# A routing stage whose low parts of weights come from adding DMAs instead of VectorE and GpSimd subtractions

## The reference, cut to what matters

```python
q = (xi @ w_pq).reshape(TOK_BLOCK, PEER_HEADS, 2, PEER_DQ // 2)
s = jnp.einsum('thcd,hckd->thck', q, sub_keys)
top_s, top_i = lax.top_k(s, PEER_TOPK)
cand_s = (top_s[:, :, 0, :, None] + top_s[:, :, 1, None, :]).reshape(TOK_BLOCK, PEER_HEADS, -1)
cand_i = (top_i[:, :, 0, :, None] * N_KEYS + top_i[:, :, 1, None, :]).reshape(TOK_BLOCK, PEER_HEADS, -1)
best_s, pos = lax.top_k(cand_s, PEER_TOPK)
idx = jnp.take_along_axis(cand_i, pos, axis=-1)
gate = jax.nn.softmax(best_s, axis=-1)
act = jax.nn.gelu(jnp.einsum('td,thkd->thk', xi, u_tab[idx]))
return jnp.einsum('thk,thkd->td', gate * act, v_tab[idx])
```

## Time and profile before

| | |
|---|---|
| median of 3 runs | 2640.74 us |
| lowest, highest | 2639.67, 2644.12 us |
| the profiled execution, its own time | 2645.87 us |
| its span in the trace | 2644.1 us |
| PE busy, share of the span | 2438.6 us, 92% |
| DVE busy | 2082.8 us, 79% |
| ACT busy | 1139.4 us, 43% |
| POOL busy | 835.4 us, 32% |
| granted TensorE clock, mean | 0.969 |

### The profile page before, as it was taken

The page is one execution under the profiler, slowest core; times in us unless marked ns, Lnnn a source line. Parts: engine busy times, 40 slices in busy tenths (PEclk is TensorE's granted clock), DMA queues, the critical chain, the costliest instruction groups (busy, mean ns, idle before and its releaser), DMA issues.

```text
span 2644.1 us, 38573 instructions
## 1 busy us (share of the span) xinstructions
PE 2438.6 (92%) x14986; PEld 2175.7 (82%) x14986; DVE 2082.8 (79%) x3567; ACT 1139.4 (43%) x1934; POOL 835.4 (32%) x559
## 2 busy tenths in 40 slices
PE   5889999998989978998995897999999999999997
PEld 4778888897878867998995786888888888888886
DVE  3667777733777674545999987999999999999999
ACT  4335565634656654324444682333333333233333
POOL 0000000003555450101464674334343334343431
PEclk9999999999999998999998898999999999999998
DMA  7421121235555555333322579999999999999996
GB/s 307 178 102 69 68 89 69 88 130 170 152 176 165 140 144 177 141 136 115 108 83 71 166 227 417 417 415 416 413 418 416 418 405 416 403 410 417 416 407 249
DMA packets 177671, 642.61 MB, mean 243 GB/s; under 512 B 15600, under 2 KB 84304, under 8 KB 117072
## 3 DMA queue, kind: packets, MB, share of 16 engines
q1 hardware_dynamic: 125680, 341.24, 34.9%
q0 software_dynamic: 36864, 268.45, 24.7%
q10 hardware_dynamic: 14944, 30.44, 4.5%
HBM read 580.23 MB, written 59.72 MB: 242 GB/s over the span
## 4 chain that ended last, share of the span: by engine, by line
PE 70%; DVE 16%; DMA 6%; issue 3%; ACT 3%; POOL 0%; SPq 0%; DVEq 0%; ACTq 0%; PEldq 0%; PEld 0%; POOLq 0%
PE c_pp L896 8%; PE p_py L2690 5%; PE p_py L2692 5%; PE p_py L2691 5%; PE p_pa L2673 4%; PE p_pa L2674 4%; PE p_pa L2675 4%; PE o_ps L1703 4%; PE e_ps L2490 4%; PE s_pg L1420 3%; DMA w_raw<-in_w_stream 3%; PE p_py L2704 3%; PE g_ps L1104 2%; PE a_ps L844 2%; DVE p_uv L2811 1%
## 5 line engine op out<-in xcount | busy, mean ns | idle before, releaser
L2655 POOL DMA_INDIRECT p_uv<-in_uv_rows,merged x256 | 402.1, 1571 | 615.9 <-DVE merged L2828 558.1
L2673 PE MATMUL p_pa<-h2D,w_hi 128*128 128x384 f32 x896 | 318.9, 356 | 20.2 <-DVE w_lo L2782 20.2
L2828 DVE SCALAR_TENSOR_TENSOR merged<-p_uv,p_sw,merged 128x1024 f32<-128x1024 f32 x256 | 328.6, 1284 | 7.8 <-DVE p_sw L2818 0.8
L2811 DVE CUSTOM_DVE_ANT_0 p_uv<-p_uv,merged 128x1024 f32<-128x1024 f32 x256 | 307.9, 1219 | 10.8 <-DMA p_uv<-in_uv_rows,merged 10.7
L2674 PE MATMUL p_pa<-h2D,w_hi 128*128 128x384 f32 x896 | 303.0, 338 | 0.0
L2675 PE MATMUL p_pa<-h2D,w_lo 128*128 128x384 f32 x896 | 303.0, 338 | 0.0
L2724 ACT ACTIVATE w_hi<-w_raw 128x2048 fp32r<-128x2048 f32 x110 | 210.3, 1912 | 153.4 <-PE p_py L2692 77.1
L2782 DVE TENSOR_TENSOR w_lo<-w_raw,w_hi 128x2048 fp32r<-128x2048 f32 x110 | 251.7, 2288 | 25.8 <-ACT w_hi L2724 25.6
L2690 PE MATMUL p_py<-w_hi,p_wh 128*128 128x512 f32 x672 | 265.7, 395 | 1.9 <-DVE w_lo L2782 1.9
L2692 PE MATMUL p_py<-w_hi,p_wl 128*128 128x512 f32 x672 | 265.3, 395 | 0.0
L2691 PE MATMUL p_py<-w_lo,p_wh 128*128 128x512 f32 x672 | 265.1, 394 | 0.0
(11 more groups left out here) (419 smaller groups left out, 5988.4 us busy)
## 6 DMA issues: line engine op xcount, KB each, us to landing
w_raw<-in_w_stream SPq DMA_DIRECT2D x174, 1024.0 KB, 8.9
g_pairs<-e_st SPq DMA_DIRECT2D x5, 4096.0 KB, 16.9
p_g<-g_pairs SPq DMA_DIRECT2D x64, 320.0 KB, 8.5
s_sums<-sum_rows ACTq DMA_DIRECT2D x38, 512.0 KB, 5.3
t_ada<-in_w_ada SPq DMA_DIRECT2D x16, 1024.0 KB, 10.3
xc_dram<-c_xc SPq DMA_DIRECT2D x8, 1284.0 KB, 5.4
p_ve<-in_v_early SPq DMA_DIRECT2D x8, 1024.0 KB, 12.9
r_ur<-in_u_early ACTq DMA_DIRECT2D x14, 512.0 KB, 3.7
```

What stands on the lines that cost most here:

```text
L2655: nc.gpsimd.indirect_dma_start(uv[:, k % RING, :], None, K.uv_rows, bass.IndirectOffsetOnAxis(K.sidx[:, t, c:c + 1], 0)).then_inc(K.gather ...
L2673: nc.tensor.matmul(ps_a[m][:, :], wh[:, k, cols], K.h2D[0][:, k, :], start=k == 0, stop=False)
L2811: nc.vector.tensor_tensor_reduce(uv[:, b, 0:D], uv[:, b, 0:D], K.hrow[:, t, :], 1.0, 0.0, ALU.mult, ALU.add, sa[:, at:at + 1]).then_inc(do ...
L2828: nc.vector.scalar_tensor_tensor(ys[:, t, :], uv[:, b, D:2 * D], sw[:, at:at + 1], ys[:, t, :], ALU.mult, ALU.add).then_inc(v_done, 1)
```

## The change

The low part is made in two steps: ScalarE writes minus the high part into the low buffer (a copy with scale -1), and a DMA that GpSimd issues adds the raw weights from DRAM onto it. That holds for the eight units from U_PQ+2 on (six for routing, two for the experts) and for all sixteen early halves. VectorE and GpSimd no longer subtract in this stage. TensorE waits for the DMA's semaphore, one per buffer. SyncE's loads from unit U_PQ+4 on wait for the high part of unit n-2 instead of its low part. GpSimd's DMAs stand in its program where its subtractions stood, the ones for the weight units between them, ahead of the look-up of the head before. At the end GpSimd waits for all adds and raises `w_lo_done` by eight, so that the stages behind see the count they expect.

```diff
--- before.py
+++ after.py
@@ -70,6 +70,7 @@
 U_O = U_SO + N_SO
 U_PQ = U_O + N_O
 U_EXP = U_PQ + N_PQ
+U_ADDED = U_PQ + 2
 N_UNITS = U_EXP + N_EXP
 
 
@@ -111,8 +112,21 @@
         self.nc.vector.tensor_tensor(K.wlo[slot][:, :], K.raw[slot][:, :], K.whi[slot][:, :].bitcast(F32),
                                      ALU.subtract).then_inc(K.w_lo_done, 1)
 
+    def minus_hi(self, act, n, slot):
+        K = self.K
+        act.wait_ge(K.w_hi_done, n + 1)
+        self.nc.scalar.activation(K.wlo[slot][:, :], K.whi[slot][:, :].bitcast(F32), ACT.Copy, scale=-1.0).then_inc(K.w_minus_done, 1)
+
+    def add_raw(self, pool, n, slot):
+        K = self.K
+        pool.wait_ge(K.w_minus_done, n - U_ADDED + 1)
+        self.nc.gpsimd.dma_start(K.wlo[slot][:, :], K.w_stream[n], accum_op=ALU.add).then_inc(K.w_added[slot], 16)
+
     def ready(self, pe, n):
         pe.wait_ge(self.K.w_lo_done, n + 1)
+
+    def ready_added(self, pe, n):
+        pe.wait_ge(self.K.w_added[n % 2], 16 * ((n - U_ADDED) // 2 + 1))
 
 
 def mm3(nc, out, lhs, rhs, first, last):
@@ -2089,7 +2103,7 @@
     LATE = range(sum(HELD), HALVES)
     low = K.merged_lo[:, :, :].rearrange("p k t -> p (k t)")
     uh, ul = ([low[:, (2 * r + m) * KD * P:(2 * r + m + 1) * KD * P].rearrange("p (k c) -> p k c", k=KD) for m in range(2)] for r in range(2))
-    uh_done = sem("r_uh_done"); ul_done = sem("r_ul_done")
+    uh_done = sem("r_uh_done"); um_done = sem("r_um_done"); ul_in = [sem("r_ul_in0"), sem("r_ul_in1")]
     ur = [sb(f"r_ur{m}", [P, KD, P]) for m in range(2)]
     ua = [sb(f"r_ua{m}", [P, TD]) for m in range(2)]
     u_in = [sem("r_u_in0"), sem("r_u_in1")]; u_mm = sem("r_u_mm"); u_ev = sem("r_u_ev"); a_out = [sem("r_a_out0"), sem("r_a_out1")]
@@ -2111,8 +2125,10 @@
         sp.dma_start(keys[:, :, :], K.keys_t).then_inc(k_in, 16)
         for i in range(2):
             load_early(sp, i)
-        for n in range(U_PQ + 3, U_PQ + 3 + PH):
-            S.load(sp, n, n % 2)
+        S.load(sp, U_PQ + 3, (U_PQ + 3) % 2)
+        for n in range(U_PQ + 4, U_PQ + 3 + PH):
+            sp.wait_ge(K.w_hi_done, n - 1)
+            sp.dma_start(K.raw[n % 2][:, :], K.w_stream[n]).then_inc(K.w_loaded[n % 2], 16)
         K.leave(sp)
 
     @block.gpsimd
@@ -2120,17 +2136,23 @@
         K.enter(pool)
         def early_lo(i):
             m = i % 2
-            pool.wait_ge(uh_done, i + 1)
-            if i >= 2:
-                pool.wait_ge(u_mm, i - 1)
-            nc.gpsimd.tensor_tensor(ul[m], ur[m][:, :, :], uh[m].bitcast(F32), ALU.subtract).then_inc(ul_done, 1)
-
-        made = lambda h: sum(HELD[:h + 1]) + 2
-        for i in range(made(0)):
+            pool.wait_ge(um_done, i + 1)
+            nc.gpsimd.dma_start(ul[m].rearrange("p k c -> p (k c)"), K.u_early[i // 2, m], accum_op=ALU.add).then_inc(ul_in[m], 16)
+
+        for i in range(2):
             early_lo(i)
+        def lows(h):
+            for i in behind_queries(h):
+                if i + 2 < HALVES:
+                    early_lo(i + 2)
+            S.add_raw(pool, h + (U_PQ + 2), h % 2)
+            for i in behind_scores(h):
+                if i + 2 < HALVES:
+                    early_lo(i + 2)
+
+        lows(0)
         for h in range(LOOKED_UP):
-            for i in range(made(h), min(made(h + 1), HALVES)):
-                early_lo(i)
+            lows(h + 1)
             pool.wait_ge(x_eq, 2 * h + 2)
             pool.wait_ge(fr_done, 2 * h + 2)
             found = eq[:, :, :, :, :].rearrange("p c t e k -> p (c t) (e k)")
@@ -2143,6 +2165,9 @@
             nc.gpsimd.tensor_tensor(slots[:, 0:2, :, TOPK * h:TOPK * (h + 1)], pair[:, :, :, 0:TOPK], pair[:, :, :, TOPK:2 * TOPK],
                                     ALU.add).then_inc(x_done, 1)
             pool.wait_ge(x_done, h + 1)
+        for s in range(2):
+            pool.wait_ge(K.w_added[s], 16 * PH // 2)
+        pool.sem_inc(K.w_lo_done, PH)
         K.clear_previous(pool)
         K.leave(pool)
 
@@ -2150,7 +2175,10 @@
     def _(pe):
         K.enter(pe)
         def queries(h, s):
-            S.ready(pe, h + U_PQ)
+            if h < 2:
+                S.ready(pe, h + U_PQ)
+            else:
+                S.ready_added(pe, h + U_PQ)
             if not (isinstance(h, int) and h == 0):
                 pe.wait_ge(q_done, 4 * h)
             wh, wl = (w[s][:, :].rearrange("p (k c) -> p k c", k=KD) for w in (K.whi, K.wlo))
@@ -2188,7 +2216,7 @@
 
         def early_hidden(i):
             m = i % 2
-            pe.wait_ge(ul_done, i + 1)
+            pe.wait_ge(ul_in[m], 16 * (i // 2 + 1))
             if i >= 2:
                 pe.wait_ge(u_ev, i - 1)
             for k in range(KD):
@@ -2255,12 +2283,13 @@
             if i >= 2:
                 act.wait_ge(u_mm, i - 1)
             nc.scalar.activation(uh[m], ur[m][:, :, :], ACT.Copy).then_inc(uh_done, 1)
+            act.wait_ge(uh_done, i + 1)
+            nc.scalar.activation(ul[m], uh[m].bitcast(F32), ACT.Copy, scale=-1.0).then_inc(um_done, 1)
 
         def early_gelu(i):
             m = i % 2
             act.wait_ge(u_mm, i + 1)
             if i + 2 < HALVES:
-                act.wait_ge(ul_done, i + 1)
                 load_early(act, i + 2)
             if i >= 2:
                 act.wait_ge(a_out[m], 16 * (i // 2))
@@ -2279,6 +2308,7 @@
                     early_hi(i + 2)
             score_copies(h, h % 2)
             S.hi(act, h + (U_PQ + 2), h % 2)
+            S.minus_hi(act, h + (U_PQ + 2), h % 2)
             for i in behind_scores(h):
                 early_gelu(i)
                 if i + 2 < HALVES:
@@ -2330,7 +2360,6 @@
                 weights(h - 1)
                 dve.wait_ge(fr_done, 2 * h)
             nc.vector.tensor_copy(f16[:, :, :, :], i16[:, :, :, :]).then_inc(f_done, 1)
-            S.lo(dve, h + U_PQ + 2, h % 2)
             dve.wait_ge(top_done, h + 1)
             top16([(cand[:, t], bv[:, t, :], ki[:, 2, t, :]) for t in range(NT)])
 
@@ -2960,6 +2989,7 @@
         K.left, K.phases_run = sem("phases_left"), 0
         K.block = ctx.enter_context(nc.Block())
         K.w_hi_done, K.w_lo_done, K.hilo_free = (sem(n) for n in ("w_hi_done", "w_lo_done", "hilo_free"))
+        K.w_minus_done, K.w_added = sem("w_minus_done"), [sem("w_added0"), sem("w_added1")]
         K.ident, K.ones, K.iota = sb("ident", [P, P]), sb("ones", [P, P]), sb("iota", [P, P])
         K.tri_le, K.tri_gt, K.tri_ge, K.tri_lt = (sb(n, [P, P]) for n in ("tri_le", "tri_gt", "tri_ge", "tri_lt"))
         K.mul1, K.add1, K.mul2, K.add2 = (sb(n, [P, KD, 2]) for n in ("mul1", "add1", "mul2", "add2"))
```

## The result

Over 20 runs of each kernel on one chip the changed kernel took a median of 2645.74 us (2638.91 to 2652.23), the kernel before 2640.07 (2636.70 to 2645.20): a ratio of 1.0021, 95% interval 1.0013 to 1.0029. It is slower by 0.21%, 5.7 us. A later set of the same program gave 1.0026 (1.0013 to 1.0038). I had forecast a gain of 3.5 us. The range held; the sign was wrong.

What follows compares the result with a forecast made beforehand. DVE's chain of eight searches was taken to bound the routing stage. Savings of 17.6 and some 6 us, less 3.0 at the start and nearly all the rest to later look-ups, left 3.5: 2640.74 to 2637.2 us, range 2629 to 2651.

Steps and rivals of the forecast that it cites:

- (c): ScalarE, each step: added negations cost 4.35 us, against 5.5 us of idle time before the next product.
- (f): DVE against POOL's look-ups: collisions cost the missing 2.0 us a head; head 7 starts at 1430.3, ends 1452.9.
- (e): Each step's second early load: issued at +13.1, 5.9 us beside the weight load; POOL's multiply 6.1 us later.
- (a): DVE, each head: one subtraction less, 8 x 2.2 = 17.6 us; a clean head takes 22.6.
- (b): POOL: sixteen subtractions gone, and with them collisions of 2.2 us each in some three places.
- (d): Start of the stage: PE 3.0 us later, 2.2 for query copies and 0.8 for the first add, landing in 5.5.
- the bounds: Gain if terms differ: 4.3 us for adds landing in 3.7, 1.6 for 7.4; 6.5 with both good ends.
- (g): Remaining adds in the steps: hidden; the second early add may take 8.3 us, the weight add is due at +35.
- rival 1: Slow adds put PE in a ring from 8.3 us of landing; at 12.1, 12 us slower, 2653; chance 0.27.
- 2, no collisions: DVE follows the score copies without meeting POOL; head 7 ends at 1445.0, 11.4 us gained, 2629; chance 0.15.
- 3, adds as costly to POOL as subtractions: Adding DMAs cost POOL 3 us or more each, or hold DVE up; gain about 1, 2640; chance 0.08.

Runs made afterwards that it cites:

- Experiment 5: experiment 1 with the first two early halves made by POOL's subtraction, as before the change; 2630.88 us, ratio 0.9960.
- experiment 1: The changed kernel with ScalarE issuing each step's second early load ahead of the weight unit's negation; 2632.13 us, ratio 0.9972.
- experiment 3: The changed kernel in halves: adding DMAs for the weight units only, 2633.22 us, 0.9973; for the early halves only, 2643.01 us, 1.0009.
- experiment 2: The changed kernel with SyncE's load of weight unit n waiting also for the add of unit n-2; 2633.67 us, ratio 0.9976.
- Experiment 6: Experiment 5 with replicas ahead of the weight copy and POOL's look-up ahead of the weight add and second early add; 2653.98 us, ratio 1.0047.
- experiment 4: experiment 1 with POOL's multiply and three sums left out of the look-ups of heads 0 to 6; 2626.83 us, ratio 0.9950.
- experiment 9: The weights-only kernel of experiment 3 with the second early load ahead of the weight unit's negation; 2630.46 us, ratio 0.9972.

## Why the prediction was wrong

The step that failed is in (c), which (f) builds on: that ScalarE keeps up with PE's step of 24.66. It was given room by a comparison of 4.35 us of work with 5.5 of idle time, and it lost the room by the term of (e), a second load of 5.9 us that measured 9.1. PE's steps became 26.7 us.

**(a) and (b), what DVE and POOL lose**: right. No DVE subtraction is left in the stage but the one ahead of the change, POOL's subtractions are gone, and a clean head lasts 22.6 (head 7, 1433.20 to 1455.90, is 22.7, of which a next head would overlap 0.1).

**(d) The start**: 3.0 forecast. In the changed kernel's profile the first query copies come 0.7 later in the stage and the second 1.2, DVE's head 1 2.0; PE waited 0.3 for the first add. But its first half had landed 1.2 earlier in the stage than before (copied at 9.1, not 10.3), and in the second profile of the same kernel the two copies are 1.6 and 3.1 late. Experiment 5 puts the whole at 2.8 of stage. That this is near 3.0 is luck. I had 2.2 for the copies and 0.8 for the first add; in experiment 1 it was 1.1 for the copies, nothing for the add, and 1.6 for TensorE's lower granted clock behind its wait (0.59 over 2.5 us), a term that I had put at nothing. The adds' landing, the unknown on which the bounds hung, measured 6.0 against my 5.5 (6.0 to 7.7 over the kernels, medians). POOL's issue took 0.87 us; 1.6 was taken.

**(e) The second early load**: this is the term that was mis-sized. The mechanism was named and its moment was right (issue at +13.1 forecast, +13.17 measured in head 1, SyncE's weight load 0.02 us away). The size was not: 5.9 us was taken from the one step of before that had the two loads together, and it took 9.1. That row had no adds beside it. The runs give the ladder: 3.7 alone; 5.9 with the weight load; 7.1 with the weight load and the weight add (experiment 3, weights only); 9.1 with the early add as well; and 4.0 to 5.1 with both adds and no weight load. The shares don't simply add up: in experiment 3's halves only there is no weight add, and beside a weight load and an early add the load took 9.2 and 8.1. So the weight load is shown to be needed (experiment 2); how the rest divides among the two adds is open, and no run took the adds' traffic away and left all else.

**(c) The negations fit into ScalarE's idle time**: this was the step that I didn't finish. I set 4.35 us of negations against 5.5 us of idle, and in (e) moved the load 2.6 us later and made it 2.2 longer, without coming back to ask when ScalarE is done. My own numbers say: 13.1+load+1.06+0.1+1.06+2.4 for the replicas, and then the table load and exponentials, 1.6: 19.3 us plus the load. With 5.9 that is 25.2, already over PE's 24.66; the limit is a load of 5.3. So even my own load made each step 0.5 longer, an estimate of 3.3 us over six steps, and nearly all of the 3.5 us of gain was gone on paper. At the measured 10.0 it gives 29.3, and the step of head 1 took 29.1. Experiment 2 lies on the other side: with loads of 4.0 to 5.1 the steps are 24.7, and ScalarE waits 1.24 for the product. So PE's step did not stay at 24.66 but became 26.7 on average (36.1 to 196.3 in six), and all that hangs on it came later: head 6's queries at 170.6 of the stage, forecast 161.3. Experiment 1 brings the steps back to 24.7 and experiment 2 four of its six, with every negation in place.

**(f) DVE settles against POOL**: right as a mechanism, and this is why the miss cost so much. DVE's head 6 started 17.6 behind that query copy, forecast 19.4, and head 7 22.7 us before its end. DVE is free to run at 22.6, but is pushed back by POOL's look-ups to the pace of PE and ScalarE: the collisions cost the difference. With steps of 24.66 that is 2.0 a head, with 26.7 it is 4.1; the 26.1 of the account are 4.35 for each of heads 1 to 6. What I missed in kind is that a late look-up also catches DVE's small operations behind the exponentials (3.17 and 2.66 us in head 1), and that DVE may wait for the exponentials themselves (4.8).

The sum then is: the end of DVE's last comparison was forecast at 228.0 of the stage (1452.9) and came at 237.2, 9.2 later, which is the 3.5 us not gained and the 5.7 lost. Head 6's queries came 9.3 later. DVE followed them 1.8 sooner than forecast, and its head 6 then took 26.3 instead of 24.66, which took this back.

**(g) The other adds are hidden**: right in the changed kernel. The second early add may take 8.3 us, and the median of the early adds is 6.0; the 1 MB add took 12.0, and 35 less 15.5 was free. Experiment 6 shows what rival 1 would be: behind a look-up and a 1 MB add the early add does end PE's waits. The Trainium skill, Collectives: The Full Stack, "The bandwidth ceiling: the fold count and why AG ≠ RS ≠ AR", says of the adding step of a collective that it reads two sources and so moves at half the rate of a copy; the trace roughly agrees (6.0 against 3.7 us for 512 KB, 12.0 for 1 MB against 4.9 for the weight loads of the stage before, the 12.0 beside other traffic), and it decided nothing.

**The rivals.** 1, the ring of slow adds, gave the right sign for a reason that did not act. That the range held is luck in the same way: its slow side was drawn for this rival. 2, no collisions: contradicted, 26.1 us of them. 3, adds as costly to POOL as subtractions: contradicted, 0.87 us. The other side deserved more chance for the reason in (c): a range of load times from 3.7 upward crosses a limit at 5.3, and beyond it ScalarE sets PE's step, which none of my bounds held. (At 9.1 the chain is 3.8 us over it; the steps grew by 2.0 on average, since behind a long step PE has its product ready and a short one follows.)

## What to carry to other kernels

When work is moved onto an engine with idle time, write out that engine's whole chain for a step, waits included, and compare its end with the step; idle time is not room if it is spent before a transfer that the change makes later. And when a release moves from one engine to another, look at which two transfers now leave together: here one load issued some 2.7 us earlier (10.5 instead of 13.2 behind the query copies) was the difference between 0.2% slower and 0.3% faster. All versions here but the halves only and experiment 6 beat both kernels (0.9960 to 0.9976, leaving out experiment 4, whose result is not the right one). Their intervals overlap, and none is shown to be the best.

## What the runs showed that I had not expected

A plain load of 512 KB took 9.1 us on average when a 1 MB load of another queue was issued with it or up to 1.2 us ahead and adds ran beside it, and about 4.5 with the adds and without that load, though over the first stretch above the DMA engines were busy only 0.63 of the time. The DVE operations that POOL's tensor operations held up include small ones and a cast with a single input: 0.24 us became 2.66. The Trainium skill, SBUF — State Buffer, "Who interferes with whom", says that casts can contend as well as instructions with two SBUF inputs, and the trace agrees; I had counted only the latter. POOL's issue of an adding DMA is no such operation: in experiment 9 five of DVE's pairs of comparisons ran across an issue (one from 1293.05, the issue at 1293.54) and lasted 1.56, as the free ones do. The most that I find beside an issue is 0.34 for 0.20, once, in the changed kernel. And TensorE's granted clock was a part of the start's cost: 1.6 of 2.7 us in experiment 1, behind a wait of 2.80 us that had been 1.70.
